# Expert weights loaded as runs of neighbouring rows, and the experts' transposes read with a matching column step

## What is computed

```python
D_MODEL, D_EXPERT, N_EXPERTS = 1024, 512, 32
def run(args):                       # one block of gathered tokens xb, all of expert e
    xb, e = args
    hdn = jax.nn.silu(xb @ w_gate[e]) * (xb @ w_up[e])   # (rows,1024) @ (1024,512), twice
    return hdn @ w_down[e]                               # (rows,512) @ (512,1024)
```

## Time and profile before

| | us |
|---|---|
| median of 3 runs | 4149.63 (4146.1 to 4149.85) |
| profiled execution | 4144.64 |
| its span, first to last instruction | 4142.9 |
| `experts`: first gate/up matmul to the end of the last block's main work | 3040.7 to 3998.7 |
| TensorE busy in the whole span | 3167.2 (76%) |

### The profile page before, as it was taken

One profiled execution on the slowest core, in us unless ns is written; L12 is line 12 of the kernel. 1 busy time (PEld: TensorE's weight loads), 2 busy tenths in 40 slices (PEclk: granted clock), 3 DMA queues, 4 the chain that ended last, 5 costly groups with the idle time before them and its releaser, 6 DMA issues. The chain is left out here.

```text
span 4142.9 us, 46437 instructions
## 1 busy us (share of the span) xinstructions
PE 3167.2 (76%) x15337; PEld 1640.7 (40%) x15338; DVE 1666.2 (40%) x3827; ACT 1135.2 (27%) x1993; POOL 824.5 (20%) x954
## 2 busy tenths in 40 slices
PE   7998959846857666777764455799569999999960
PEld 3544433533437534545542333455223333333320
DVE  1163776756732378887633222133300000000015
ACT  1131535513411258874440001011001111111111
POOL 1412211201213143223313222000210001011114
PEclk9999989867755587898987777899789999999985
DMA  4101010002221111100006432333067767786757
GB/s 169 53 18 56 16 43 18 28 13 75 80 53 51 41 38 28 40 24 16 11 15 162 130 84 75 109 104 112 32 211 267 250 227 260 256 287 230 255 177 260
DMA packets 237846, 452.97 MB, mean 109 GB/s; under 512 B 51801, under 2 KB 89785, under 8 KB 237452
## 3 DMA queue, kind: packets, MB, share of 16 engines
q1 hardware_dynamic: 195276, 340.02, 24.5%
q0 software_dynamic: 29152, 89.50, 7.3%
q10 hardware_dynamic: 13280, 21.77, 1.7%
HBM read 364.45 MB, written 86.74 MB: 109 GB/s over the span
## 5 line engine op out<-in xcount | busy, mean ns | idle before, releaser
L729 PE MATMUL pj_cm<-pj_xT,pj_w 128*64 128x512 f32 (+3 forms) x1520 | 434.6, 548 | 6.5 <-DVE pj_xT L410 5.8
L2747 PE MATMUL ex_pgu<-ex_wgu,ex_xT 128*64 128x512 f32 x1344 | 297.7, 595 | 0.0
L2747 PE MATMUL ex_pgu<-pre_wgu,ex_xT 128*64 128x512 f32 x1312 | 292.5, 598 | 0.7 <-ACT ex_xT L2667 0.7
L729 PEld LDWEIGHTS pj_cm<-pj_xT,pj_w 128*64 128x64 f32 (+1 forms) x1520 | 191.9, 185 | 241.0 <-issue 230.1
L2712 DVE TENSOR_TENSOR ex_hid<-ex_sg,ex_pgu 128x256 f32<-128x256 f32 x83 | 35.0, 421 | 596.4 <-ACT ex_sg L2671 596.4
L1953 PE MATMUL ap_SB<-keep_kT,ap_qs 64*128 64x512 f32 (+3 forms) x640 | 173.3, 635 | 99.7 <-DVE ap_m L1885 79.5
L1964 PE MATMUL ap_TB<-keep_const,ap_L 128*128 128x128 f32 x1088 | 177.0, 306 | 69.4 <-ACT ap_PT L1746 47.0
L1734 ACT ACTIVATE ap_L<-ap_L,ap_nm 128x128 f32<-128x128 f32 (+15 forms) x128 | 153.1, 1197 | 178.2 <-DVE ap_nm L1890 174.6
L656 ACT ACTIVATE pj_U<-pj_sc,pj_cand 128x512 bf16<-128x512 f32 (+4 forms) x155 | 183.3, 1183 | 64.9 <-DVEq L491 64.6
L470 DVE TENSOR_SCALAR_CACHE_REDUCE pj_U<-pj_sc,pj_cand 128x384 bf16<-128x384 f32 (+9 forms) x182 | 194.8, 1103 | 14.2 <-issue 0.5
L1964 PEld LDWEIGHTS ap_TB<-keep_const,ap_L 128*128 128x128 f32 x1088 | 130.1, 153 | 150.0 <-ACT ap_L L1734 61.8
(11 more groups left out here) (474 smaller groups left out, 5362.0 us busy)
## 6 DMA issues: line engine op xcount, KB each, us to landing
pre_wgu<-in_w_gate SPq DMA_DIRECT2D x16, 2048.0 KB, 9.4
pre_wgu<-in_w_up SPq DMA_DIRECT2D x16, 2048.0 KB, 14.9
pre_down_wd<-in_w_down SPq DMA_DIRECT2D x16, 2048.0 KB, 8.9
ex_wgu<-in_w_gate SPq DMA_DIRECT2D x16, 2048.0 KB, 9.3
ex_wgu<-in_w_up SPq DMA_DIRECT2D x16, 2048.0 KB, 14.8
ex_wd<-in_w_down SPq DMA_DIRECT2D x16, 2048.0 KB, 8.9
yslot<-ex_y ACTq DMA_DIRECT2D x166, 128.0 KB, 6.1
pj_x<-in_x_prompt SPq DMA_DIRECT2D x16, 512.0 KB, 5.2
```

The lines of the kernel that those rows point to most:

```text
L729: mm = pe.matmul(cm[u % 2][cols * n:cols * n + cols, 0:width_], w[:, k, c0:c0 + cols], xT[:, k, 0:width_], start=(k == 0), stop=(k == KD - 1))
L2747: mm = pe.matmul(pgu[BR * t:BR * t + BR, :], xT[:, k % 4, k // 4, :], wgu[par][:, k, :, 256 * t:256 * t + 256], start=(k == 0), stop=(k == ...
```

## The change

Weight rows are stored differently: a partition takes runs of neighbouring rows. For gate and up, half h and slot k of partition p hold row 512h + 4p + k (k = 0 to 3), so that a partition reads two runs of 8 KB. For down it is row 256h + 2p + k (k = 0, 1), also two runs of 8 KB. The gate/up buffer is laid out with gate and up outermost, so that the run is contiguous in SBUF too.

The activations follow: the transposes of `xg` take every fourth column (a step of 16 bytes) in place of 128 neighbouring ones, those of `hid` every second column (8 bytes). The matmuls of `gate_up` read gate and up from places 16 KB apart in the partition, 2 KB apart before, 256 columns from each.

```diff
 def load_gate_up(sp, io, buf, e, sem):
     for n, name in enumerate(("w_gate", "w_up")):
-        sp.dma_start(buf[:, :, n, :], io[name][0, e].rearrange("(k p) f -> p k f", p=P)).then_inc(sem, 16)
+        sp.dma_start(buf[:, n].rearrange("p (h k) f -> p h (k f)", h=2), io[name][0, e].rearrange("(h p k) f -> p h (k f)", h=2, k=4)).then_inc(sem, 16)
 
 def load_down(sp, io, buf, e, sem):
-    sp.dma_start(buf[:], io["w_down"][0, e].rearrange("(k p) f -> p k f", p=P)).then_inc(sem, 16)
+    sp.dma_start(buf[:].rearrange("p (h k) f -> p h (k f)", h=2), io["w_down"][0, e].rearrange("(h p k) f -> p h (k f)", h=2, k=2)).then_inc(sem, 16)
...
-        wgu = [keep["ew_gu"], a.sb("wgu", [P, KD, 2, DE])]
+        wgu = [keep["ew_gu"], a.sb("wgu", [P, 2, KD, DE])]
...
             def turn_rows(b):
                 pe.wait_ge(sm["xg_in"], 16 * b + 16)
                 for k in range(4):
-                    mm = pe.transpose(tp[:, k * P:(k + 1) * P], xg[:, k * P:(k + 1) * P], ident)
+                    mm = pe.transpose(tp[:, k * P:(k + 1) * P], xg[:].rearrange("p (j k) -> p k j", k=4)[:, k, :], ident)
...
                         mm = pe.matmul(pgu[BR * t:BR * t + BR, :], xT[:, k % 4, k // 4, :],
-                                       wgu[par][:, k, :, 256 * t:256 * t + 256], start=(k == 0), stop=(k == KD - 1))
+                                       wgu[par][:, :, k, 256 * t:256 * t + 256], start=(k == 0), stop=(k == KD - 1))
...
             def turn_hidden(b):
                 pe.wait_ge(sm["hid_ok"], b + 1)
                 for k in range(2):
-                    mm = pe.transpose(ph[:, k * P:(k + 1) * P], hid[:, k * P:(k + 1) * P], ident)
+                    mm = pe.transpose(ph[:, k * P:(k + 1) * P], hid[:].rearrange("p (j k) -> p k j", k=2)[:, k, :], ident)
...
-            keep["ew_gu"], keep["ew_gu_in"], keep["ew_d_in"] = b.sb("wgu", [P, KD, 2, DE]), b.sem("ew_gu_in"), b.sem("ew_d_in")
+            keep["ew_gu"], keep["ew_gu_in"], keep["ew_d_in"] = b.sb("wgu", [P, 2, KD, DE]), b.sem("ew_gu_in"), b.sem("ew_d_in")
```

## The result

| | before | after |
|---|---|---|
| median of 15 runs each, us | 4149.85 | 4172.28 |
| profiled span, us | 4142.9 | 4174.7 |
| period of a block of `experts`, us | 11.56 | 11.72 |

The ratio of the times is 1.0047, with an interval of [1.0032, 1.0063]: the changed kernel is slower by 19.5 us (13 to 26); the two medians lie 22.4 us apart. The forecast was +12.1 us. The two profiled executions lie 31.8 us apart, more than the medians. 8.5 us of that had already come about before `attend_sample`, in stages that the change doesn't touch. Most of it is one pause early in the sample scores, 5.8 us in this execution of the kernel before and 12.1 us in this one of the kernel after.

A forecast was written before the change was run, and what follows sets the result against it. The prediction took TensorE to bound the experts, busy 957.62 of 958 us with no wait for weights. Its terms, 8.1 + 0.4 + 0 + 2.6 + 1.0 = +12.1 us on 4149.6, gave 4162 us, range 4149 to 4172.

The forecast's parts named there:

- `xg`, step of 16 bytes: Transposes of `xg` in the experts' blocks: stepped weight loads set the pace, 0.098 us a block, 8.1 us in all.
- `hid`, step of 8 bytes: Transposes of `hid` in the experts' blocks: step nearly free, 0.005 us a block, 0.4 us; upper bound 6.3 us.
- Gate and up 16 KB apart: Gate/up matmuls of the experts: the larger jump between the two runs of 256 columns costs 0.
- The wait for keys: Sample attention, beside expert 0's load: larger weight packets lengthen TensorE's wait by 2.6 us, bounds -2.9 and +5.
- First gather: First gather of the experts, issued into a running load: 1.0 us later, between -3.5 and +1.8.
- both steps cost the full price: Rival: transposes of `xg` and `hid` cost 8.1 and 6.3 us, +18.0 in all, 4168 us; chance 0.12.
- The steps are free: Rival: stepped transposes in the experts cost nothing, only the transfers show, +3.6, 4153 us; chance 0.12.
- not slower: Rival: larger pieces shorten the waits at the keys and first gather, steps are free, 4143 us; chance 0.07.
- the pieces stay small: Rival: the descriptors cut the weight loads small again, so only the steps cost, 4158 us; chance 0.03.

The follow-up runs named there:

- xg_step2: The kernel before, with the transposes of `xg` reading every second column (8 bytes), sums not kept; one run, 4152.93 us.
- loads_only: The changed kernel's 8 KB loads and weight layout, with the transposes of the kernel before, sums not kept; ratio to the kernel before 1.0007, +2.9 us.
- no_steps: The changed kernel with DVE writing `xn` and `hid` already sorted, so no transpose reads with a step; ratio to the kernel before 1.0013, +5.4 us.
- steps_only: The kernel before, its loads kept, with the changed kernel's stepped transposes of `xg` and `hid`, sums not kept; ratio 1.0033, +13.7 us.
- hid_by_dve: The changed kernel, but DVE writes `hid` already sorted, so only `xg` is read with a step; one run, 4161.04 us.

## Why the prediction came out as it did

The direction and the main cause were right: slower, by the steps in TensorE's own stream, with nothing won by the faster loads. The size was short: +12.1 forecast, +19.5 measured (13 to 26). The ratio on the median before gives 4169 us, inside the range; the median of the runs itself, 4172.28, lies at its upper end, 0.3 us beyond. That the range holds the time is owed to the harsher bounds which it included, the full price for `hid` above all, and not to the terms of the forecast. Term by term:

- **`xg`, step of 16 bytes:** forecast 0.098 us a block (8.1 us), measured 0.094 (7.8 us), with 0.69 us from start to start as foretold. The row of another stage, on 32 partitions, carried over to 128. That row takes 0.119 us at either granted clock; that the cause is how SBUF hands out the columns, as the prediction says, was argued and not tested. Nor does a run show what fills the last 0.09 us of the four transposes, which the prediction put down to the array's change of shape; it doesn't enter the sum.
- **`hid`, step of 8 bytes:** the first step that failed. Forecast 0.005 us a block (0.4 us), measured 0.070 (5.8 us), which is near the upper bound, 0.076, that stood in the range as 6.3 us. The argument was that 0.119 us is 128 separate places and that every second column touches only 64. `xg_step2` refutes it: in one and the same tile both steps cost alike. For steps of two, three and four numbers, what counts is that the columns read are not neighbours in memory, and hardly how many of them fall in one piece of 16 bytes; larger steps were not run. The Trainium skill's rule (SBUF — State Buffer, Door 1: The DMA port swizzle, the note on "cachelines") made the 8-byte step free as well. Measured here it isn't, for LDWEIGHTS of float32.
- **Gate and up 16 KB apart:** 0, as forecast.
- **The wait for keys:** the second step that failed, +2.6 forecast, 30.9 - 25.4 = +5.5 measured in the wait itself, just beyond the bound of +5. Two things were wrong. The present cost was read as 2.9 us, against one neighbour of 22.84 us; waits without a load scatter from 18 to 24 us, their mean is about 20.5, and the cost is 4.9. That neighbour was one of the four longest of the sixty. The factor of 0.32 / 0.17 = 1.9 was right in size, 10.4 / 4.9 = 2.1. That was luck: it had been reasoned from turns of whole pieces, two of 2 KB to a turn, and 16 KB, which would have doubled the cost again, doesn't follow that. Some of the 5.5 may be given back in the next wait, which is 1.5 us shorter with 8 KB; that is within the scatter of single waits. By ratios, the loads add 2.9 us in `loads_only`, 5.4 in `no_steps`, and the step from `steps_only` to the kernel after is 0.0014, 5.8 us.
- **First gather:** +1.0 forecast, +0.1 measured on this pair of profiles (7.45 and 7.55 us). Over four profiles each it is 6.6 to 7.5 us at 2 KB and 7.6 at 8 KB, means 7.1 and 7.6, so +0.5. The size of the pieces matters little; that there is a load at all costs about 4 us.

The sum with the measured terms is 13.6 + 5.5 + 0.1 = 19.2 us against 19.5. So close an agreement is partly chance, with an interval of 13 to 26 and single waits that scatter by more than 1 us; only the first term is known better than that. The two misses point the same way, since both took the mild reading where the harsher bound was at hand. Of the rivals, "both steps cost the full price" was the case that came, and its 4168 is close to the 4169 of the ratio. "The steps are free", "not slower" and "the pieces stay small" are excluded by the block of 11.72 us, by the wait of 31.50 us and by the packets of 0.31 us.

## What to carry to other kernels

Read first who waits for a transfer: a more efficient load is worth nothing under an engine that is busy all the time, and what it adds to that engine's own stream is paid in full, once a block, here 0.164 us each time. Where a large load shares the queues with a small transfer that is waited for, its place matters more than the size of its pieces; moving two loads gained 7.5 us, while reshaping all of them gained nothing. And take the cost of one disturbed wait against the mean of several undisturbed ones, not against its neighbour.

## What the runs showed of the hardware

- LDWEIGHTS of 128 float32 columns: the next load starts 0.06 us later when the columns are neighbours, and 0.11 to 0.12 us later with a step of 8, 12 or 16 bytes. Beside a matmul of 128 streamed columns (0.11 us) the difference shows only in part: 0.094 us over four transposes, 0.070 over two.
- A DVE instruction that writes by turns to two places 512 bytes apart pays too: 617 ns in place of 421 for 128 x 256 float32 numbers, with its inputs read in order (`hid_by_dve`).
- A packet took 0.085, 0.164 and 0.31 us for 2, 4 and 8 KB, so the larger pieces saved 8% of the DMA engines' time for gate and up.
- A load beside gathered keys made their wait 4.9, 5.7, 10.4 and 11.7 us longer with pieces of 2, 4, 8 and 16 KB (4.4, 4.9, 10.0 and 12.6 us counted from the gather's issue). The figures for 4 and 16 KB are one wait each. The jump between 4 and 8 KB was not expected and is not explained.
